# The position bias in the second attention: from TensorE to VectorE

## The chip, the cores and the metric

The kernel runs on one NeuronCore of a Trainium2 chip. The metric is the time of one execution on the device in microseconds (us). PE is TensorE, DVE is VectorE, ACT is ScalarE, POOL is GpSimd and SP is SyncE. PEld is the weight load of TensorE.

## The reference

One step of a two-layer diffusion backbone in fp32: 128 context tokens and 256 latent tokens (a grid of 4 rows by 64), width 1024. Layer 0 mixes tokens by differential attention, layer 1 by neighbourhood attention with 16 heads of 64; each is followed by an output projection, a layer norm, and a mixture of experts (32 experts, two per token). What matters here is the softmax of layer 1 for the latent tokens:

```
s_nb = einsum('bqhd,biqjhd->bhqij', q_r, k_nb) * scale
s_nb = s_nb + bias                       # learned, by head and offset; the window is 16 columns wide
s_ctx = einsum('bqhd,bphd->bhqp', q_r, k_ctx) * scale
p = softmax(concatenate([s_nb, s_ctx], -1))
```

The context tokens of that layer attend only to each other, without a bias.

## The kernel before, in words

All five engines have an instruction list written out by hand, and semaphores order them; no planner is at work. The stages follow each other: modulation, QKV projection, attention, output projection, layer norm, routing, experts; then layer 1 the same way.

Attention runs over 24 units, a unit being one tile of 128 queries and one pair of heads: `u // 8` is the tile `t` (0 the context, 1 and 2 the latent tokens), `u % 8` the pair `j`. A unit of tile 0 has 128 keys, one of tiles 1 and 2 has 384: the 128 of the context first, then the 256 latent ones. The 16 units of tiles 1 and 2 in layer 1 (`l == 1`) are the ones with a bias.

TensorE (`block.tensor`) issues, after three scores ahead, for each unit `u`: `transpose_prob(u)` (L787), `scores(u + 3)` (L769, and L776 for the bias), `attend(u - 1)` (L802, probabilities times values). The scores of both heads lie in two PSUM banks, and there are two such pairs of banks, so `scores(u)` waits for the exponentials of unit `u - 2`. In layer 1 the six transposes of a unit go into banks 4 and 5, which are not doubled: `transpose_prob(u)` waits until ACT has copied those of `u - 1` out. An fp32 matmul appears in the trace as two records, a transpose as one.

For the bias, PE multiplies the identity (`ident`) with a table `btab` in SBUF that holds, for every head, six runs of 64 columns: the bias shifted to its place and a very large negative number outside the window. It accumulates onto the scores of the latent keys, columns 128 to 384 of each bank. The table is made earlier in the layer (PE flips it, DVE adds the window at L1053).

DVE (`block.vector`) issues `maxima(u + 1)` (wait for the scores, then the negated maximum over the keys of both heads, L1067) and then `combine(u)`, which in layer 1 is only the reciprocal of the sums (L1077). When `u % 4 == 1` and `u >= 5` it issues `take_o`, which waits for the values matmuls of four units and writes half of an output tile (L1094). `chain(x)` issues x on DVE and then a drain, so that the next instruction of DVE starts only when x has written.

ACT (`block.scalar`) issues `exps(u + 2)` (two exponentials with their sums, L587; they wait for the maximum and for `transpose_prob(u)`, whose source buffer they overwrite) and then `take_pT(u)` (the transposed probabilities from PSUM to SBUF, L600). On POOL and SP nothing of the attention stage is waited for except that POOL loads the layer norm's rows when the last values matmul is done.

Of the kernel before, what the change touches and what calls it, by code (L numbers as in the profile page):

```python
# [20 lines left out]
P = 128  # L21
# [5 lines left out]
HD = 64  # L27
# [18 lines left out]
GRID_W = 64  # L46
NA_KH, NA_KW = 8, 16
ROWS = 256 // GRID_W
BM = 6
# [11 lines left out]
ALU = mybir.AluOpType  # L61
# [44 lines left out]
def backbone_kernel(nc, x_prompt, x_sample, cache_a_k, cache_a_v, cache_b_k, cache_b_v, c, c_ctx,  # L106
# [4 lines left out]
    with ctx:  # L111
# [3 lines left out]
        def overlay(tensors):  # L115

            with ExitStack() as s:
                return [s.enter_context(nc.sbuf_tensor(n, shape, dt)) for n, shape, dt in tensors]
# [4 lines left out]
        def sem2(name):  # L123
# [34 lines left out]
        qkv, hT, qT, kT, kctx, vctx, o = overlay([  # L158
            ("qkv", [P, NT, 3 * D], F32), ("hT", [P, KD, NT * P], F32), ("qT", [P, KD, NT * P], F32),
            ("kT", [P, KD, 4 * P], F32), ("kctx", [P, D], F32), ("vctx", [P, D], F32), ("o", [P, NT, D], F32)])  # L160
# [22 lines left out]
        ps = ps_t[:, :].rearrange("p (b n) -> p b n", b=8)  # L183
# [5 lines left out]
        ident = cst[:, C_ID:C_ID + P]  # L189
# [55 lines left out]
        def qkv_chunk(l, c):  # L245

            return QKV_B + c if l else QKV_A + c + 2 * min(c, KD)
# [11 lines left out]
        keys = [P, 3 * P, 3 * P]  # L259
        key0 = [0, P, P]  # L260
# [378 lines left out]
        def _(pe):  # L639
            mm = nc.tensor.matmul  # L640
# [57 lines left out]
            for kk in range(4):  # L698
                ins = nc.tensor.transpose(ps[:, 7, kk * P:(kk + 1) * P], mst[:, 0, kk * P:(kk + 1) * P], ident)
            ins.then_inc(mt_ps, 1)  # L700

            for l in range(LAYERS):
# [8 lines left out]
                for g in range(3):  # L711
# [3 lines left out]
                    for ck in range(4):  # L715
                        n = qkv_chunk(l, 4 * g + ck)
# [5 lines left out]
                    if l == 1 and g < 2:  # L722

                        pe.wait_ge(hank_ld, 32 * (g + 1))
                        for i in range(6):
                            f = 6 * g + i
                            if f >= 2:
                                pe.wait_ge(flip_used, f - 1)
                            mm(ps[:, 6 + f % 2, :], cst[:, C_FLIP:C_FLIP + P], hank[:, i * 512:(i + 1) * 512],
                               start=True, stop=True).then_inc(flip_done, 1)  # L730
# [8 lines left out]
                for j in range(PAIRS):  # L739
# [4 lines left out]
                    for t in range(NT):  # L744
                        ins = nc.tensor.transpose(ps[:, bq, t * P:(t + 1) * P], qkv[:, t, j * P:(j + 1) * P], ident)
# [3 lines left out]
                    for i in range(4):  # L749
                        ins = nc.tensor.transpose(ps[:, bk, i * P:(i + 1) * P], kin[i], ident)  # L750
# [11 lines left out]
                def scores(u):  # L762
                    t, j = u // PAIRS, u % PAIRS
                    if u >= 2:

                        pe.wait_ge(exp_done[l], u - 1)
                    biased = l == 1 and t > 0
                    for h in range(2):
                        ins = mm(ps[:, 2 * (u % 2) + h, 0:keys[t]],  # L769
                                 qT[HD * h:HD * (h + 1), j, t * P:(t + 1) * P],  # L770
                                 kT[HD * h:HD * (h + 1), j, key0[t]:key0[t] + keys[t]], start=True, stop=not biased)
                    if biased:
                        m0 = (2 - 2 * (t - 1)) * GRID_W
                        for h in range(2):
                            at = (2 * j + h) * BM * GRID_W + m0
                            ins = mm(ps[:, 2 * (u % 2) + h, P:keys[t]], ident, btab[:, at:at + ROWS * GRID_W],  # L776
                                     start=False, stop=True)
                    ins.then_inc(sc_done[l], 1)

                def transpose_prob(u):  # L780
# [25 lines left out]
                for u in range(3):  # L806
                    scores(u)
                for u in range(UNITS):
                    transpose_prob(u)
                    if u + 3 < UNITS:  # L810
                        scores(u + 3)
                    if u:
                        attend(u - 1)
# [5 lines left out]
                for cidx, nk in enumerate(WO_K):  # L819
                    n = WO0[l] + cidx  # L820
# [17 lines left out]
                for t in range(NT):  # L838
                    for k in range(KD):
                        ins = mm(ps[:, 6, t * w36:(t + 1) * w36], hT[:, k, t * P:(t + 1) * P], wr[:, l, k, :],  # L840
                                 start=(k == 0), stop=(k == KD - 1))
# [8 lines left out]
                for t in range(NT):  # L850
                    for i in range(t + 1):
                        mm(ps[:, 7, t * NE:(t + 1) * NE], tri if i == t else ones, a_all[:, i, :],
                           start=(i == 0), stop=(i == t))
                for t in range(NT):
                    ins = mm(ps[0:NE, 5, 0:1], a_all[:, t, :], ones[:, 0:1], start=(t == 0), stop=(t == NT - 1))
# [15 lines left out]
                for i in range(2 * NT):  # L871
                    ins = mm(ps[:, 1, 0:NBX], rt[:, 2400 + i * P:2400 + (i + 1) * P],
                             rt[:, 3200 + i * NBX:3200 + (i + 1) * NBX], start=(i == 0), stop=(i == 2 * NT - 1))
# [42 lines left out]
                with pe.Fori(0, n_act // HALVES) as pair:  # L916
                    for half in range(HALVES):
                        at = pair * HALVES + half
# [9 lines left out]
        def _(dve):  # L928
            v = nc.vector

            def chain(ins):

                dve.drain()
                return ins
# [90 lines left out]
            for l in range(LAYERS):  # L1025
# [35 lines left out]
                def maxima(u):  # L1061

                    t, j = u // PAIRS, u % PAIRS
                    n = keys[t]
                    sc = ps[:, 2 * (u % 2):2 * (u % 2) + 2, :]
                    dve.wait_ge(sc_done[l], u + 1)
                    v.tensor_reduce(negm[:, u % 2, :], sc[:, :, 0:n], AX, ALU.max, negate=True).then_inc(negm_rdy[l], 1)  # L1067

                def combine(u):
# [32 lines left out]
                def head_norm(q, step):  # L1102
# [17 lines left out]
                    else:  # L1120
                        chain(v.tensor_tensor(oh, oh, subg[:, :].unsqueeze(1).to_broadcast([P, 4, P]), ALU.mult))
                        if half:
                            dve.sem_inc(o_rdy[l], 1)

                maxima(0)
                for u in range(UNITS):
                    if u + 1 < UNITS:
                        maxima(u + 1)
                    combine(u)
                    q = (u - 5) // 4  # L1130
                    if u >= 5:
                        if u % 4 == 1:
                            take_o(q)
                        if l == 0:

                            for step in range(2 * ((u - 1) % 4), min(2 * ((u - 1) % 4) + 2, 7)):
                                head_norm(q, step)
# [214 lines left out]
```

## Time and profile before

| what | value |
|---|---|
| time, median of 3 runs | 1601.62 us (1598.58 to 1602.39) |
| the profiled execution's own time | 1598.8 us |
| its span, first to last instruction | 1597.0 us |
| mean granted TensorE clock | 0.853 of full |
| PE busy | 1110.6 us, 70% of the span |
| DVE busy | 404.2 us, 25% |
| ACT busy | 170.1 us, 11% |

Busy is the time in which the engine executed something; a granted clock of 1.00 is 2.4 GHz, 0.50 is 1.2 GHz. The second attention lies at about 988 to 1071 us of the span, the first at about 200 to 283. Times in rows are counted from the start of the span.

### The profile page before, as it was taken

The numbers are of one execution on the slowest core, as the hardware profiler recorded it, in microseconds if no ns is written. First come the engines' busy times: TensorE is split into PE (matmuls) and PEld (weight loads), VectorE is DVE, ScalarE is ACT, GpSimd is POOL, SyncE is SP. The second block draws the span as 40 slices with busy tenths as digits, with TensorE's granted clock in tenths as the row PEclk, the third lists the DMA queues.
The fourth block names the chain that finished last, engine by engine and source line by source line (L and its number), as shares of the span: only waits on it lengthen the run. The fifth ranks groups of instructions, "written<-read, shape, count | busy, mean of one in ns | idle before, by whom it ended". The sixth has DMA issues, their size and how long they took to land.

```text
span 1597.0 us, 25857 instructions
## 1 busy us (share of the span) xinstructions
PE 1110.6 (70%) x9606; PEld 587.1 (37%) x9607; DVE 404.2 (25%) x906; ACT 170.1 (11%) x460; POOL 210.9 (13%) x359
## 2 busy tenths in 40 slices
PE   3899977888448767865219998999426577877720
PEld 1333444424224433432114445774323234443310
DVE  0011177354201111110091112322741011111116
ACT  0110143001000000000000003440000000000000
POOL 0000000000112322331100000000002122322220
PEclk9899967896679988997659998899559689998975
DMA  8776300287699999999914423010039999699830
GB/s 330 267 263 251 94 25 1 103 311 311 267 423 388 424 423 426 381 425 424 422 56 141 123 79 105 1 51 3 40 133 409 424 426 424 246 423 384 359 150 40
DMA packets 84327, 398.26 MB, mean 249 GB/s; under 512 B 14656, under 2 KB 14944, under 8 KB 56640
## 3 DMA queue, kind: packets, MB, share of 16 engines
q1 hardware_dynamic: 61136, 341.91, 52.9%
q0 software_dynamic: 16240, 53.09, 9.1%
q10 hardware_dynamic: 6912, 2.76, 0.6%
q8 instruction: 22, 0.36, 0.1%
q14 instruction: 17, 0.14, 0.0%
HBM read 381.12 MB, written 16.72 MB: 249 GB/s over the span
## 4 chain that ended last, share of the span: by engine, by line
PE 44%; DMA 37%; DVE 10%; issue 3%; ACT 2%; DVEq 1%; SPq 1%; POOL 0%; ACTq 0%; POOLq 0%
PE ps L684 21%; DMA ring<-in_w_down_dram 20%; DMA ring<-in_w_up_dram 10%; PE ps L893 6%; PE ps L911 4%; DMA ring<-in_w_ada_dram 2%; PE ps L802 2%; DMA qkv<-ybuf 2%; PE ps L660 2%; PE ps L769 2%; DMA x<-in_x_sample_dram 1%; PE ps L840 1%; PE ps L787 1%; PE ps L776 1%; DMA ring<-in_w_gate_dram 1%
## 5 line engine op out<-in xcount | busy, mean ns | idle before, releaser
L893 PE MATMUL ps<-ring,xs 128*32 128x256 f32 x4736 | 313.9, 420 | 142.6 <-DMA ring<-in_w_up_dram 89.1
L893 PEld LDWEIGHTS ps<-ring,xs 128*32 128x32 f32 x4736 | 175.8, 119 | 273.1 <-issue 200.1
L684 PE MATMUL ps<-ring,hT 128*128 128x512 f32 x576 | 255.4, 604 | 5.3 <-ACT hT L536 4.2
L911 PE MATMUL ps<-ring,hm 128*32 128x256 f32 x2368 | 150.9, 393 | 36.7 <-ACT hm L630 27.1
L684 PEld LDWEIGHTS ps<-ring,hT 128*128 128x128 f32 x576 | 110.8, 194 | 148.8 <-issue 141.0
L1294 DVE TENSOR_TENSOR hp<-sg,ps 128x128 f32<-128x128 f32 x74 | 21.3, 288 | 330.1 <-ACT sg L627 330.1
L911 PEld LDWEIGHTS ps<-ring,hm 128*32 128x32 f32 x2368 | 69.4, 112 | 95.9 <-ACT hm L630 41.6
L1302 DVE COPY yo<-ps 128x256 f32<-128x256 f32 x74 | 31.4, 425 | 240.3 <-DMA ybuf<-yo,idy 161.4
L684 PE MATMUL ps<-ring,qT 128*128 128x512 f32 x192 | 84.9, 605 | 2.3 <-ACT qT L559 2.3
L627 ACT ACTIVATE sg<-ps 128x128 f32<-128x128 f32 x74 | 20.5, 277 | 616.0 <-PE ps L893 616.0
L451 POOL DMA_INDIRECT xg<-xmod,idx x78 | 77.3, 991 | 61.7 <-POOL idx L448 60.9
L461 POOL DMA_INDIRECT ybuf<-yo,idy x74 | 73.9, 999 | 61.1 <-POOL idy L458 58.2
L675 PE MATMUL ps<-cst,qkv 128*128 128x128 f32 x72 | 14.6, 376 | 79.7 <-DVE qkv L1013 55.1
L660 PE MATMUL ps<-ring,cond 128*32 128x512 f32 x384 | 53.6, 681 | 14.7 <-DMA ring<-in_w_ada_dram 14.7
L448 POOL COPY idx<-toki 128x1 int32 (+1 forms) x78 | 14.3, 183 | 364.9 <-DVE xs L1289 275.9
L900 PE MATMUL ps<-cst,hp 128*128 128x128 f32 x74 | 24.8, 335 | 52.9 <-DVE hp L1294 50.7
L587 ACT ACTIVATE hT<-ps,negm 128x384 f32<-128x384 f32 (+1 forms) x96 | 48.0, 505 | 83.7 <-DVE negm L1067 57.1
L684 PEld LDWEIGHTS ps<-ring,qT 128*128 128x128 f32 x192 | 37.2, 195 | 48.9 <-issue 46.1
L769 PE MATMUL ps<-kT,qT 64*128 64x384 f32 (+1 forms) x192 | 47.3, 582 | 4.0 <-ACT hT L587 2.3
L787 PE MATMUL ps<-cst,hT 128*128 128x128 f32 x168 | 33.7, 324 | 21.1 <-DVE hT L1085 18.2
L1289 DVE STREAM_TRANSPOSE xs<-xg 128x256 f32<-128x256 f32 x76 | 33.8, 445 | 55.7 <-DMA xg<-xmod,idx 55.5
L802 PE MATMUL ps<-qkv,hT 128*128 128x64 f32 (+1 forms) x240 | 46.6, 323 | 0.0
(194 smaller groups left out, 833.2 us busy)
## 6 DMA issues: line engine op xcount, KB each, us to landing
ring<-in_w_gate_dram SPq DMA_DIRECT2D x82, 1024.0 KB, 15.0
ring<-in_w_up_dram SPq DMA_DIRECT2D x82, 1024.0 KB, 15.2
ring<-in_w_down_dram SPq DMA_DIRECT2D x82, 1024.0 KB, 15.2
ring<-in_w_ada_dram SPq DMA_DIRECT2D x48, 1024.0 KB, 8.9
ring<-in_w_qkv_a_dram SPq DMA_DIRECT2D x12, 1024.0 KB, 5.1
ring<-in_w_qkv_b_dram SPq DMA_DIRECT2D x12, 1024.0 KB, 11.8
modb<-mdram POOLq DMA_DIRECT2D x12, 512.0 KB, 8.8
qkv<-ybuf POOLq DMA_DIRECT2D x2, 3072.0 KB, 15.6
```

The source lines that it names most:

```text
L451: pool.indirect_dma_start(out=xg[:, :], out_offset=None, in_=xmod.rearrange("r (j w) -> (r j) w", j=G), in_offset=bass.IndirectOffsetOnAxi ...
L461: pool.indirect_dma_start(out=ybuf.rearrange("r (j w) -> (r j) w", j=G), out_offset=bass.IndirectOffsetOnAxis(ap=idy[:, 0:1], axis=0), in_ ...
L587: ins = act.activation(e[:, h, 0:n], ps[:, 2 * (u % 2) + h, 0:n], ACT.Exp, bias=negm[:, u % 2, h:h + 1], accum_out=sums[:, u % 2, h:h + 1])
L660: ins = mm(ps[j * BLK:(j + 1) * BLK, ADA_BANK[i], :], cond[:, k, :], raw[:, n % RING, j * 512:(j + 1) * 512], start=False, stop=(k == KD - 1))
L684: ins = mm(ps[:, 2 * t + hf, :], lhs[:, k, t * P:(t + 1) * P], raw[:, slot, kk * D + hf * 512:kk * D + (hf + 1) * 512], start=(k == 0), st ...
L769: ins = mm(ps[:, 2 * (u % 2) + h, 0:keys[t]], qT[HD * h:HD * (h + 1), j, t * P:(t + 1) * P], kT[HD * h:HD * (h + 1), j, key0[t]:key0[t] + ...
L787: ins = nc.tensor.transpose(ps[:, 4 + (u % 2 if l == 0 else h), i * P:(i + 1) * P], prob[u % 2][:, h, i * P:(i + 1) * P], ident)
L802: ins = mm(tile_ps(3)[:, lo:lo + w], probT[u % 2][:, h, i * P:(i + 1) * P], values(t, i, lo, lo + w), start=(i == 0), stop=(i == nk - 1))
L893: ins = mm(ps[j * BLK:(j + 1) * BLK, 1, 0:W].rearrange("p (a n) -> p a n", a=2), xs[:, k, :], w[:, :, at:at + FW], start=(k == 0), stop=(k ...
L911: ins = mm(ps[j * BLK:(j + 1) * BLK, 5, 0:WD], hm[:, 2 * c + q, :], ring[:, slot + GU + c, q * D + j * WD:q * D + (j + 1) * WD], start=(c ...
L1289: v.transpose(xs[:, :, :].rearrange("p k n -> p (k n)"), xg[:, :]).then_inc(xs_rdy[l], 1)
L1302: v.tensor_copy(yo[:, :], ps[:, 5, 0:WD]).then_inc(yo_rdy[l], 1)
```

## The change

The matmuls with the identity go, and the matmul of the scores closes its own accumulation. DVE adds the same part of the table to the same columns of both banks, in place in PSUM, with one instruction for both heads, and drains before it takes the maximum.

```
@@ scores(u), TensorE
-                    biased = l == 1 and t > 0
                     for h in range(2):
                         ins = mm(ps[:, 2 * (u % 2) + h, 0:keys[t]],
                                  qT[HD * h:HD * (h + 1), j, t * P:(t + 1) * P],
-                                 kT[HD * h:HD * (h + 1), j, key0[t]:key0[t] + keys[t]], start=True, stop=not biased)
-                    if biased:
-                        m0 = (2 - 2 * (t - 1)) * GRID_W
-                        for h in range(2):
-                            at = (2 * j + h) * BM * GRID_W + m0
-                            ins = mm(ps[:, 2 * (u % 2) + h, P:keys[t]], ident, btab[:, at:at + ROWS * GRID_W],
-                                     start=False, stop=True)
+                                 kT[HD * h:HD * (h + 1), j, key0[t]:key0[t] + keys[t]], start=True, stop=True)
                     ins.then_inc(sc_done[l], 1)
@@ maxima(u), VectorE
                     dve.wait_ge(sc_done[l], u + 1)
+                    if l == 1 and t > 0:
+                        m0 = (2 - 2 * (t - 1)) * GRID_W
+                        bias = btab[:, 2 * j * BM * GRID_W:2 * (j + 1) * BM * GRID_W].rearrange("p (h n) -> p h n", h=2)
+                        chain(v.tensor_tensor(sc[:, :, P:n], sc[:, :, P:n], bias[:, :, m0:m0 + ROWS * GRID_W], ALU.add))
                     v.tensor_reduce(negm[:, u % 2, :], sc[:, :, 0:n], AX, ALU.max, negate=True).then_inc(negm_rdy[l], 1)
```

## Rows read from the trace of the kernel before

**Rows 1.** Busy time of each engine by stretch: us, (x instructions), PEclk, DMA share, GB/s.

```profile
core 0: us, PE busy (x) PEld busy (x) DVE busy (x) ACT busy (x) POOL busy (x), PEclk, DMA share, GB/s
1018.00:1034.00 16.00, 15.85 (x107) 12.40 (x106) 4.81 (x9) 7.80 (x21) 0.00 (x0) 1.00 0.01 1
1050.00:1070.70 20.70, 18.74 (x145) 16.19 (x143) 3.95 (x8) 9.35 (x22) 0.00 (x0) 1.00 0.00 1
```

**Rows 2.** The chain of waits through one plain unit: start us, us, what.

```profile
1022.25 0.66 PE ps L787 x6
1022.91 0.85 PE ps L769 x4
1023.75 1.06 PE ps L776 x4
1024.82 1.28 PE ps L802 x12
```

**Rows 3.** Groups of instructions, 1000 to 1072 us: busy, mean ns, idle before, releasers.

```profile
L776 PE MATMUL ps<-btab,cst 128*128 128x256 f32 x64 | 19.0, 422 | 0.0
L1067 DVE TENSOR_REDUCE negm<-ps 128x2 f32<-128x768 f32 x16 | 15.3, 958 | 27.0 <-PE ps L776 26.3 <-issue 0.4
```

**Rows 4.** The chain of waits around the output at 1045 us.

```profile
1042.42 0.85 PE ps L769 x4
...
1045.65 0.69 DVE o L1094
1046.34 0.03 DVEq L1097
...
1046.54 0.97 DVE negm L1067
...
1048.77 0.71 ACT hT L600
1049.47 0.14 issue
1049.61 0.84 PE ps L787 x6
1050.45 0.85 PE ps L769 x4
```

**Rows 5.** The timeline: start us, us, engine, instruction, [idle before, releaser].

```profile
1024.85 0.96 DVE L1067 TENSOR_REDUCE negm<-ps 128x2 f32<-128x768 f32 x1 [2.82 <-PE ps L776]
...
1050.55 0.58 ACT L587 ACTIVATE hT<-ps,negm 128x384 f32<-128x384 f32 x1 [1.09 <-PE ps L787]
...
1051.68 0.81 ACT L600 ACTIVATE hT<-ps 128x768 f32<-128x768 f32 x1
```

**Rows 6.** DVE groups by shape over the span, then two chained instructions of the timeline.

```profile
L1053 DVE TENSOR_TENSOR btab<-ps,cst 128x512 f32<-128x512 f32 x12 | 8.3, 692 | 84.4 <-PE ps L729 84.3
L1094 DVE TENSOR_TENSOR o<-ps,rsum 128x512 f32<-128x512 f32 x12 | 8.3, 691 | 29.5 <-PE ps L802 29.5
L1007 DVE TENSOR_TENSOR qkv<-t,modb 128x1024 f32<-128x1024 f32 x6 | 11.6, 1926 | 0.5
...
225.81 0.69 DVE L1109 TENSOR_TENSOR t<-o 128x512 f32<-128x512 f32 x1
226.58 0.69 DVE L1111 TENSOR_REDUCE var<-t 128x4 f32<-128x512 f32 x1
```

**Rows 7.** The chain of waits through the first biased units.

```profile
1001.45 1.58 PE ps L769 x4
1003.03 2.00 PE ps L776 x4
...
1008.95 0.85 PE ps L769 x4
...
1014.93 0.85 PE ps L769 x4
```

**Rows 8.** Busy time by stretch again: the first attention, and the start of the biased units.

```profile
204.00:286.00 82.00, 63.19 (x263) 39.89 (x263) 64.35 (x180) 33.54 (x112) 2.08 (x4) 0.69 0.02 7
...
258.00:262.00 4.00, 1.75 (x11) 1.02 (x11) 3.22 (x13) 1.61 (x5) 0.00 (x0) 1.00 0.00 0
...
266.00:270.00 4.00, 3.13 (x12) 1.43 (x10) 3.56 (x9) 2.37 (x8) 0.00 (x0) 0.50 0.00 0
...
1006.00:1008.00 2.00, 2.00 (x9) 1.23 (x9) 0.10 (x2) 1.51 (x5) 0.00 (x0) 0.84 0.00 0
```

## Prediction

> **What bounds the kernel now.** I read the chain of waits for the stretch of the second attention first, then the busy time of the engines by stretch, then the groups of instructions, and last the timeline where the chain leaves TensorE. The stretch that the change touches runs from the first biased scores at 1001.45 us [rows 7] to 1070.7. In it PE is busy for 15.85 of 16.00 us from 1018 and 18.74 of 20.70 from 1050, DVE for 4.81 and 3.95, DMA for next to nothing [rows 1]. The chain stays on PE: transposes of the probabilities 0.66, scores 0.85, bias 1.06, values 1.28 us, so one unit (a head pair of a query tile) takes 3.85 us [rows 2]. DVE only waits there: 26.3 us until the bias matmuls end [rows 3]. The reader should see that PE is the bound of a plain unit, that the other engines have slack, and that every fourth unit the chain leaves PE for DVE and ACT [rows 4].
>
> **What goes.** 32 matmuls with the identity, recorded as 64 (two for each), 19.0 us of PE records at 422 ns [rows 3]. Records overlap, so I price by the chain: 1.06 us per unit at full clock, 2.00 us for the first unit, which runs at half [rows 2, 7]. Sixteen units: 2.0 + 15 x 1.06 = 17.9 us of PE time. That is the ceiling, not the gain. Their weight loads go too; they lie beside the matmuls.
>
> **What comes.** Sixteen in-place adds of 128 x 512 on DVE, ahead of the maximum, with a drain between. No row shows a DVE instruction that reads and writes PSUM. The nearest, 512 elements from PSUM plus SBUF into SBUF, takes 692 ns, and so does the one of L1094 [rows 6]. Below that nothing speaks for less. From above I take the dearest two-operand form by its elements: 1926 ns for 1024 with a broken-up pattern [rows 6] is 0.96 us for 512. I take 0.69, since both operands here run in two straight pieces. With the drain the maximum starts 226.58 - 225.81 = 0.77 us after the add [rows 6]. Sixteen of them are 12.3 us of DVE time, in an engine with over 10 of 16 us idle. What matters is only how late the maximum becomes.
>
> **A plain unit afterwards.** PE alone would need 0.66 + 0.85 + 1.28 = 2.79 us. But a second loop is close behind. The transposes of a unit wait for the copy that ACT made of the previous unit's; ACT's exponentials for two units on wait for those transposes, since they reuse the buffer; and the copy stands behind the exponentials on ACT. One turn can be read where the chain passes through it: the copy ends at 1048.77 + 0.71 = 1049.48, PE begins to transpose at 1049.61 [rows 4], ACT begins the exponentials at 1050.55 and ends the next copy at 1051.68 + 0.81 = 1052.49 [rows 5]. So 3.01, say 3.02 us. A plain unit saves 3.85 - 3.02 = 0.83 us, not 1.06. Does the add fit? Count from the start of the scores: they end at 0.85, DVE starts 0.03 later (24.82 + 0.03 [rows 2, 5]), 0.77 for the add, 0.96 for the maximum [rows 5], 0.03 to ACT: 2.64. ACT wants it 3.02 + 0.10 = 3.12 after the start of the scores (1050.55 against 1050.45 [rows 4, 5]). Slack 0.48 us, so the add costs nothing here, also at the upper bound of 0.96 us. Queued behind it on DVE are only the reciprocal and, every fourth unit, the output of the sums.
>
> **Every fourth unit.** DVE then takes the output half from PSUM (0.69 us), waiting for the values matmuls of a unit ago, and the next maximum stands behind it [rows 4]. Before, the start of that wait is 0.85 + 1.06 + 1.28 = 3.19 after the scores, the maximum ends 1.86 after DVE begins (1045.65 to 1047.51), and the next scores but one start late by little: 1050.45 - 1042.42 = 8.03 against 7.70, a loss of 0.33 us. After, the wait ends at 0.85 + 1.28 = 2.13; 0.03 and 0.69 for the output, 0.20 until DVE is free (1046.54 - 1046.34), 0.77 and 0.96 for add and maximum, 0.03 to ACT: 4.81, where ACT wanted it at 3.12. The loop has no slack of its own, so these 1.69 us are all on the path: the unit takes 4.71 instead of 4.18. Each costs 0.53 us against before. This is the wait that takes the place of the matmuls.
>
> **Sum.** I count intervals between the starts of the scores of two units; the biased ones are 8 to 23. From unit 13 on there are eight plain intervals: 8 x 0.83 = 6.6; and two with an output: 2 x -0.53 = -1.1. The first four intervals (units 8 to 12, 1001.45 to 1014.93, 13.48 us [rows 7]) still have short transposes and values; the last two take 5.98, so 2.99 us each, and run at the ACT loop already. In the first, at half clock, the bias is in the way for 2.00 us; I give 1.8, less a little for the second. The interval after it, with the first output, gains 0.3 by the same walk (clock and buffers are as before), and the tail with the last output 0.2. Together 6.6 - 1.1 + 1.8 + 0.3 + 0.2 = 7.8 us at an unchanged clock. The add at its upper bound takes 0.27 more at four outputs: 6.7.
>
> **The clock.** The granted clock is half, 1.2 GHz, when the biased units begin; the first scores take 1.58 us instead of 0.85. It rises to 2.4 GHz in 1006 to 1008 (mean 0.84 [rows 8]), and is 1.00 from 1018 on, where PE is busy almost without gaps [rows 1, 7]. Afterwards PE would be busy for 4 x 2.79 = 11.2 of 4 x 3.02 + 1.69 = 13.8 us, 81%, with a gap at each output. In the first attention PE was busy for 63.19 of 82.00 us and its clock was 0.69 on average, so half for (1 - 0.69) / 0.5 = 62% of the time: full from 258 to 262 with PE busy for 1.75 us, half from 266 to 270 with 3.13 [rows 8]. On the other side 1050 to 1070.7 kept the full clock with PE idle for 2.0 us. At half, a unit takes about 2.79 x 1.58 / 0.85 = 5.2 us instead of 3.02, so each us at half loses 0.42. I take 4 to 5 us more at half than before (a rise that comes a little later, or one fall), 1.9 us, and keep 0 and 6 us of loss for the range. The page "TensorE: Matmul & The Clock Gate" of the Trainium skill, section "A second HAM failure mode: psum-queue depth-cycling", says that short idle spells of the PE between groups of matmuls can make its clock swing between the levels. By that rule the second attention would become like the first, and the change would be slower. The first attention agrees with that rule, the stretch from 1050 to 1070.7 does not [rows 1, 8].
>
> **After the attention** nothing hides the gain: the output projection and all that follows wait for its end in series, DMA is idle in the stretch [rows 1], and the weights of that projection do not keep it waiting. So 7.8 - 1.9 = 5.9 us reach the end. The profiled execution took 1598.8 us, 1.8 more than its span of 1597.0; it becomes 1592.9. The median of the runs shown is 1601.62, 2.8 above; I forecast for it: 1595.7 us.
>
> **Rivals.** (1) The clock is lost. Place: from the second biased unit to the end. For it: the first attention [rows 8], the gap of about 1.7 us at every output, and the place of the change: the removed matmuls ran just where the clock rose. Against: 81% busy is more than in the first attention. It decides from 7.8 / 0.42 = 19 us more at half. With 30 us, most of what the stretch then lasts for, it costs 12.6 - 7.8 = +4.8: 1606.4. Chance 0.15. (2) DVE becomes the bound because in-place access to PSUM is dear, say twice the nearest row, 1.38 us. Then ACT wants the maximum 0.21 us sooner than it comes in eight plain units, and at four outputs it comes 0.69 later still: 7.8 - 1.7 - 2.8 = 3.3, less 1.9 for the clock: 1600.2. Against: every plain DVE form of 512 elements lies at 0.69. Chance 0.12. (3) PE was the only bound and the ACT loop is looser than I read: 8 x 0.23 = 1.8 more, 1593.9 or less. Against: the turn was read at one place, but without a gap in it. Chance 0.08. (4) The change doesn't do what it says, PE being off the path: against it stand the chain and 26.3 us of DVE waiting; 1601.6, chance 0.03.
>
> **How the numbers follow.** The forecast has 0.62, its own range 1592.5 to 1599.5. The whole range, 1590.5 to 1603, takes in the lower loss of clock with the looser loop, and the dear add; it leaves out most of the first rival. What a measurement can tell from no change is 0.3%, 4.8 us, that is below 1596.8 for faster. The forecast is faster in about three of four cases; with rival 3 and little of the others: 0.54. Slower than 1606.4 is the worse half of the first rival, and a little of unknown causes: 0.09. The rest, 0.37, is the same.
>
> **What would show it.** Right: score starts 3.0 us apart in plain units with the exponentials following the transposes without a wait for DVE; 4.7 us at outputs, with ACT waiting for the maximum; the add at 0.69 us; sixteen DVE adds and no bias matmuls. Wrong: half clock in the stretch beyond 1012 us for more than a few us, adds well over 0.7 us, or plain units at 2.8 or at 3.3 and more.

## The result: slower by 0.4%, and the profile after

The changed kernel takes 1607.09 us (median of 20 runs, 1602.27 to 1612.03), the kernel before 1600.88 (20 runs, 1593.63 to 1607.38). The ratio is 1.0042, 95% interval 1.0028 to 1.0057: 6.2 us slower, where 5.9 us faster were forecast. It is the first rival, given 0.15 and 1606.4 us.

The profiled execution: span 1603.1 us, against 1597.0. First the busy time by stretch, for the kernel before over the stage from its first biased scores to its last values (us, busy and (x instructions) of PE, PEld, DVE, ACT, POOL, then the granted clock, DMA share and GB/s).

```profile
1001.45:1070.68 69.23, 66.98 (x438) 52.73 (x439) 20.20 (x40) 32.77 (x87) 0.00 (x0) 0.96 0.01 1
```

The same view of the kernel after: the stage, and the stretches that answer to those before [rows 1, 8].

```profile
998.12:1075.10 76.98, 72.17 (x374) 54.43 (x374) 31.40 (x56) 32.77 (x87) 0.00 (x0) 0.70 0.00 1
...
204.00:286.00 82.00, 58.70 (x272) 36.74 (x272) 66.34 (x188) 34.99 (x120) 2.08 (x4) 0.77 0.03 11
...
1003.00:1018.00 15.00, 15.00 (x58) 10.45 (x59) 7.42 (x13) 5.64 (x17) 0.00 (x0) 0.50 0.01 2
1018.00:1034.00 16.00, 14.33 (x96) 10.20 (x95) 8.31 (x14) 9.07 (x25) 0.00 (x0) 0.93 0.00 1
1034.00:1050.00 16.00, 16.00 (x64) 11.80 (x63) 5.18 (x9) 4.29 (x12) 0.00 (x0) 0.50 0.00 1
1050.00:1070.70 20.70, 17.56 (x127) 15.19 (x125) 7.78 (x14) 10.98 (x27) 0.00 (x0) 0.91 0.00 1
```

The stage is 7.75 us longer. PE executes 64 records fewer in it (374 for 438) and is busy for 5.2 us longer. The reader should see the granted clock: 0.70 for 0.96. A mean of 0.70 is (1 - 0.70) / 0.5 = 60% of 77 us at half, 46 us; before it was 8% of 69, 5.5 us. (The first attention, whose code is the same, went from 0.69 to 0.77; in the fourteen traces of this case it lies between 0.67 and 0.77, so it varies by itself.) From 1034 to 1050 PE is busy for 16.00 of 16.00 us, and all of it at 1.2 GHz: a full row of PE is not a sign that PE works at its rate.

Now the chain of waits after, which answers to the plain unit and to the output before [rows 2, 4]: a plain unit at full clock, the output, and a unit at half clock.

```profile
1021.44 0.84 PE ps L768 x4
1022.28 1.48 PE ps L795 x12
1023.76 0.69 PE ps L780 x6
1024.46 0.84 PE ps L768 x4
...
1026.82 0.69 DVE o L1091
...
1027.64 0.70 DVE ps L1063
...
1028.41 0.97 DVE negm L1064
...
1030.63 0.71 ACT hT L600
1031.34 0.14 issue
1031.48 0.85 PE ps L780 x6
1032.32 0.93 PE ps L768 x4
1033.25 2.75 PE ps L795 x12
1036.00 1.28 PE ps L780 x6
1037.28 1.58 PE ps L768 x4
1038.87 2.75 PE ps L795 x12
```

L768 are the scores, L795 the values, L780 the transposes. At full clock the scores are 1024.46 - 1021.44 = 3.02 us apart. At half they are 2.75 + 1.28 + 1.58 = 5.61 apart, where the kernel before needed 3.85 with the bias in them. The clock fell just behind the output, about 1.5 us after PE had waited 1.67 us. Now the tail, behind the last output. The busy time by stretch after, with PE idle for 2.71 us and then at half clock:

```profile
1063.00:1067.00 4.00, 1.29 (x13) 1.19 (x12) 1.04 (x3) 2.13 (x6) 0.00 (x0) 1.00 0.00 0
1067.00:1071.00 4.00, 4.00 (x22) 4.00 (x22) 0.00 (x0) 1.42 (x2) 0.00 (x0) 0.51 0.00 0
```

The chain of waits from the last values to the first matmul of the output projection (L684), before and then after:

```profile
1068.06 2.63 PE ps L802 x24
...
1074.56 5.85 PE ps L684 x13
```

```profile
1070.09 5.01 PE ps L795 x24
...
1080.03 4.99 PE ps L684 x11
```

The half clock runs on behind the stage: from its end to the projection are 1080.03 - 1075.10 = 4.9 us, where they were 1074.56 - 1070.68 = 3.9. Last, the new DVE group, over the span.

```profile
L1063 DVE TENSOR_TENSOR ps<-ps,btab 128x512 f32<-128x512 f32 x16 | 11.2, 700 | 18.2 <-PE ps L768 17.4 <-issue 0.4
```

### The profile page after: what moved, and what is told of

Its sections match the earlier page's. It is cut to its first block, busy times and chain, and to the rows that moved or that the text cites. A ratio compares the mean times of both kernels' runs of the same rounds, so it can differ in the third digit from the quotient of the medians.

```text
span 1603.1 us, 25761 instructions
## 1 busy us (share of the span) xinstructions
PE 1116.5 (70%) x9542; PEld 586.7 (37%) x9543; DVE 415.3 (26%) x922; ACT 170.3 (11%) x460; POOL 211.0 (13%) x359
## 4 chain that ended last, share of the span: by engine, by line
PE 45%; DMA 36%; DVE 10%; issue 3%; ACT 2%; DVEq 1%; SPq 1%; POOL 0%; ACTq 0%; POOLq 0%
PE ps L684 21%; DMA ring<-in_w_down_dram 17%; DMA ring<-in_w_up_dram 12%; PE ps L886 7%; PE ps L904 4%; PE ps L795 3%; DMA ring<-in_w_ada_dram 2%; DMA qkv<-ybuf 2%; PE ps L660 2%; PE ps L768 2%; DMA x<-in_x_sample_dram 1%; PE ps L780 1%; PE ps L833 1%; DVE negm L1064 1%; DVEq L926 1%
## 5 line engine op out<-in xcount | busy, mean ns | idle before, releaser
L886 PE MATMUL ps<-ring,xs 128*32 128x256 f32 x4736 | 319.9, 426 | 139.5 <-DMA ring<-in_w_up_dram 86.2
L684 PE MATMUL ps<-ring,hT 128*128 128x512 f32 x576 | 254.2, 602 | 5.3 <-ACT hT L536 4.2
L684 PEld LDWEIGHTS ps<-ring,hT 128*128 128x128 f32 x576 | 110.3, 193 | 148.1 <-issue 140.3
L1291 DVE TENSOR_TENSOR hp<-sg,ps 128x128 f32<-128x128 f32 x74 | 21.3, 288 | 333.2 <-ACT sg L627 333.2
L684 PE MATMUL ps<-ring,qT 128*128 128x512 f32 x192 | 84.7, 603 | 2.2 <-ACT qT L559 2.2
L780 PE MATMUL ps<-cst,hT 128*128 128x128 f32 x168 | 37.0, 351 | 26.8 <-DVE hT L1082 20.9
L684 PEld LDWEIGHTS ps<-ring,qT 128*128 128x128 f32 x192 | 37.0, 194 | 48.9 <-issue 46.0
L795 PE MATMUL ps<-qkv,hT 128*128 128x64 f32 (+1 forms) x240 | 53.2, 358 | 0.0
L768 PE MATMUL ps<-kT,qT 64*128 64x384 f32 (+1 forms) x192 | 49.9, 610 | 4.0 <-ACT hT L587 2.3
L795 PEld LDWEIGHTS ps<-qkv,hT 128*128 128x128 f32 x240 | 45.1, 262 | 10.3 <-issue 10.2
```

The source lines that it names most:

```text
L684: ins = mm(ps[:, 2 * t + hf, :], lhs[:, k, t * P:(t + 1) * P], raw[:, slot, kk * D + hf * 512:kk * D + (hf + 1) * 512], start=(k == 0), st ...
L768: ins = mm(ps[:, 2 * (u % 2) + h, 0:keys[t]], qT[HD * h:HD * (h + 1), j, t * P:(t + 1) * P], kT[HD * h:HD * (h + 1), j, key0[t]:key0[t] + ...
L780: ins = nc.tensor.transpose(ps[:, 4 + (u % 2 if l == 0 else h), i * P:(i + 1) * P], prob[u % 2][:, h, i * P:(i + 1) * P], ident)
L795: ins = mm(tile_ps(3)[:, lo:lo + w], probT[u % 2][:, h, i * P:(i + 1) * P], values(t, i, lo, lo + w), start=(i == 0), stop=(i == nk - 1))
L886: ins = mm(ps[j * BLK:(j + 1) * BLK, 1, 0:W].rearrange("p (a n) -> p a n", a=2), xs[:, k, :], w[:, :, at:at + FW], start=(k == 0), stop=(k ...
```

## Experiments

Two questions were open: is the loss the clock, or the longer way through DVE; and if it is the clock, is it the gap of PE at the outputs or the smaller amount of PE work. "Stage" below is from the first biased scores to the last values, in the one profiled execution. Ratios are to the kernel before in the same series, whose medians were 1602.18 and 1602.27 us.

**The changed kernel, two more profiled executions.** No edit.

> The changed kernel once more, one look, to see how far its clock differs from one execution to the next. Theory CLOCK: half for a good part of the stage again, mean granted clock 0.6 to 0.85 in it, stage 68 to 80 us, and the units at full clock 3.02 us apart, those at half 5.6. A clock of 0.95 with a stage of 77 us would be against it.

> The changed kernel a third time, one look: a mean clock of 0.6 to 0.85 in the stage and falls that follow outputs, at other outputs than in the two looks so far; stage 68 to 80 us.

Measured: 1611.60 and 1612.32 us; stages of 74.2 and 74.8 us at a mean clock of 0.78 and 0.75, so 33 and 37 us at half. Both are in the expected ranges. One expectation failed: the falls came at no other outputs than before. In all three executions one followed the second output of the stage and one the last; one of the three had a fall at the third as well. In the first of the two, the busy time by stretch around two outputs and what came behind them (columns as above):

```profile
1032.00:1036.00 4.00, 2.33 (x19) 1.97 (x18) 3.09 (x6) 1.93 (x5) 0.00 (x0) 1.00 0.00 0
1036.00:1042.00 6.00, 6.00 (x27) 4.57 (x27) 1.73 (x3) 2.25 (x6) 0.00 (x0) 0.55 0.00 0
1052.00:1056.00 4.00, 3.42 (x17) 2.31 (x17) 1.60 (x4) 2.37 (x6) 0.00 (x0) 0.71 0.00 0
1056.00:1060.00 4.00, 4.00 (x17) 2.83 (x16) 0.54 (x2) 1.18 (x5) 0.00 (x0) 0.50 0.01 4
```

The gap comes first, then the half clock, with PE busy all the time.

**The kernel before, a second profiled execution.** No edit.

> The kernel before once more, one look, for the spread of its stage: clock 0.93 to 0.97 and 69 to 71 us expected.

Measured: 69.1 us, clock 0.97. The three stages after, 77.0, 74.2 and 74.8, have a mean of 75.3; less 69.2 that is 6.1 us. With the 1.1 us behind the stage (4.9 for 3.9 in all three, against both of the kernel before) it is 7.2, and the medians differ by 6.2, with an interval of 4.5 to 9.1. So no other cause is needed, though three executions can't exclude one of a microsecond or two: in the same changed kernel the stage begins at 998.1, 1004.5 and 1004.8 us, and nothing ahead of it was changed. The 6.1 us lie in two places. Up to the last scores the stage is 2.5 us longer (59.1 for 56.6), and from the last scores to the last values 3.7 us (16.3 in each of the three, for 12.6 in both).

**Filler in the place of the bias matmuls.**

```
# scores(u), l == 1 and t > 0, ahead of the scores
+   for h in range(2):
+       for _ in range(2):
+           mm(ps[:, 2 * (u % 2) + h, 384:512], ident, btab[:, 384:512], start=True, stop=True)
```

> Edit: the changed kernel, and ahead of the scores of each biased unit PE again runs as many columns through the identity as the removed bias matmuls had (two of 128 columns for each head), but into the 128 spare columns of the scores' bank, which nothing reads. DVE still adds the bias. Theory CLOCK (the removed matmuls had kept PE busy enough for the full clock; without them it falls to half): the granted clock is as in the kernel before, 0.9 or more over the stage from the first biased scores to the last values, plain units are 3.85 us again, outputs cost about 0.75 us more each than before; stage 71 to 73 us against 69.2 before and 77.0 after; time 1602 to 1605, below the changed kernel although PE does more. Theory DVE (the add in front of the maximum is what costs): the stage stays at 77 or gets longer, time 1607 or more.

Measured: 1613.22 us (12 runs), ratio 1.0054 (1.0034 to 1.0074); stage 74.6 us at a clock of 0.93. The clock went as the clock theory said and the units too: 3.88 us plain, 4.88 and 4.96 with an output, against 4.10 and 4.18 before. The time did not: it is no better than the changed kernel. The miss of the stage is in its tail, 17.2 us from the last scores to the last values for 12.6 before. Behind the last output PE idled and the clock was lost here too:

```profile
1063.00:1067.00 4.00, 1.27 (x11) 1.16 (x11) 1.67 (x4) 1.93 (x5) 0.00 (x0) 0.98 0.00 0
1067.00:1071.00 4.00, 4.00 (x21) 4.00 (x20) 0.00 (x0) 0.81 (x1) 0.00 (x0) 0.50 0.00 0
```

Two parts lie outside the stage: the projection begins 1.7 us later behind it, at half clock, and the filler of the first biased unit runs ahead of it, where the context units take 15.6 us for 13.9. Together 5.4 + 1.7 + 1.7 = 8.8 us over the kernel before; the ratio says 8.6 (5.4 to 11.9).

So the add on DVE costs something at the outputs whatever the clock does, 0.78 us each, and a clock that is held by work in the way of the scores is paid for with that work. This run alone doesn't decide between the two theories.

**The output one maximum later.**

```
# DVE, the loop over units
-   if u >= 5:
-       if u % 4 == 1:
+   if l == 1 and u >= 6 and u % 4 == 2:
+       take_o(q)
+   if u >= 5:
+       if l == 0 and u % 4 == 1:
            take_o(q)
```

> Edit: the changed kernel, with the output half in the second attention taken one maximum later, so that the maximum no longer queues behind it on DVE. The gap of PE at every fourth unit should go. Theory CLOCK: with the gaps gone the clock should not fall once it is full, so the stage is 77 less 4 x 1.7 and less what the half clock after the gaps took: 60 to 68 us, time 1592 to 1600; if the clock stays at half for long even without gaps, what it looks at is how much PE works in a unit and not the gaps, and the stage is 70 or more. Theory DVE queue (the wait behind the output is all of the loss): 4 x 1.7 = 6.8 us less, stage 70, time 1600, with the clock as in the changed kernel.

> The changed kernel with the output one maximum later once more, one look: if no gap means no fall, again every full-clock unit at 3.02 us, no half clock after the first rise, stage 56 to 59 us.

Measured: 1590.63 us (6 runs), ratio 0.9919 (0.9891 to 0.9948), and 1595.97 in the second profiled execution, beside one of the kernel before at 1603.82. The stages are 57.25 and 57.2 us at a clock of 0.90 in both, for the first of them less than either theory expected. The chain of waits of the first, where an output now lies inside:

```profile
1030.22 0.85 PE ps L768 x4
1031.07 1.48 PE ps L795 x12
1032.55 0.69 PE ps L780 x6
1033.24 0.85 PE ps L768 x4
1034.09 1.48 PE ps L795 x12
1035.57 0.70 PE ps L780 x6
1036.27 0.85 PE ps L768 x4
1037.11 1.48 PE ps L795 x12
1038.59 0.70 PE ps L780 x6
1039.29 0.85 PE ps L768 x4
```

Every unit takes 3.02 us and the chain never leaves PE. The busy time by stretch of the same run: half until the clock rises, then full to the end.

```profile
1004.75:1016.00 11.25, 11.25 (x39) 6.29 (x38) 5.55 (x10) 5.17 (x19) 0.00 (x0) 0.50 0.01 2
1018.00:1062.00 44.00, 42.99 (x326) 34.39 (x325) 23.94 (x43) 26.79 (x67) 0.00 (x0) 1.00 0.01 1
```

The stage is 18 us shorter than the mean of the changed kernel. The delay at four outputs explains at most 4 x 1.9 = 7.6 (4.93 - 3.02 at the longest); the rest is the clock. This is also the version that beats both kernels.

**The same order in the kernel before.**

> Edit: the kernel before (bias by PE matmuls), with the output half in the second attention taken one maximum later. It asks how much of the gain of the late output belongs to the order alone. Theory GAPS (the late output gains where it closes gaps that let the clock fall; before, there are hardly any): three intervals lose 0.33, 0.25 and 0.28 us and the tail 1 us; stage 67 to 68.5 us, time 1599 to 1601. Theory ORDER (taking the output later is worth 10 us in any kernel): 1592.

Measured: 1600.38 us (12 runs), ratio 0.9982 (0.9960 to 1.0005); stage 67.5 us, clock 0.96. This is what theory GAPS expected. The order alone is worth at most some 6 us and likely 2. The gain of 12 to 13 us over the kernel before belongs to the two changes together.

**Filler in the gaps only.** Nothing of the delay is taken away.

```
# PE, the loop over units, behind attend(u - 1)
+   if l == 1 and u >= 9 and u % 4 == 1:
+       at = ((u - 1) % PAIRS + 1) * P
+       for _ in range(3):
+           mm(tile_ps(3)[:, at:at + 3 * P], ident, btab[:, 0:3 * P], start=True, stop=True)
```

> Edit: the changed kernel, the order of DVE untouched; PE fills its gap at each of the four outputs with three matmuls of the identity over 384 spare columns of the output bank, about 1.3 us at full clock, which nothing reads. The wait of ACT for the maximum stays. Theory CLOCK BY GAPS: the clock no longer falls after an output; it still begins at half, so 65 to 72 us for the stage and 1598 to 1603 in time, 4 to 9 less than the changed kernel. Theory DELAY (the maximum behind the output costs the time itself, idle PE does not matter): the filler changes nothing or adds to the path, 1607 to 1612.

Measured: 1597.98 us (12 runs), ratio 0.9971 (0.9946 to 0.9995); stage 64.7 us, clock 0.91. The output units still take 4.97 to 4.98 us. (The filler was sized wrong: it takes 2.15 us at full clock, not 1.3, so it overfills the gap.) Twelve matmuls that compute nothing make the changed kernel 9 us faster by the medians and 11 by the two ratios; the stage is 10.6 us shorter. The delay theory wanted 1607 or more. The busy time by stretch:

```profile
1000.00:1010.00 10.00, 10.00 (x36) 5.78 (x36) 4.85 (x9) 4.87 (x15) 0.00 (x0) 0.50 0.01 2
1010.00:1062.67 52.67, 51.95 (x360) 39.64 (x360) 25.41 (x44) 26.83 (x68) 0.00 (x0) 1.00 0.00 1
```

**Filler in the context units**, to begin at full clock: alone, with the filler in the gaps, and with the late output.

```
# scores(u), l == 1 and t == 0, ahead of the scores
+   for h in range(2):
+       mm(ps[:, 2 * (u % 2) + h, 128:512], ident, btab[:, 128:512], start=True, stop=True)
```

> Edit: the changed kernel, and ahead of the scores of the eight context units of layer 1 (no bias, 128 keys) PE runs the identity over 384 spare columns of each of the two banks, which nothing reads. Theory CLOCK: the clock is full when the biased units begin (it is half there before and after), the context stage takes no longer than its 13 us, and the first biased units run at 3.0 us; outputs still open gaps, after which it may fall. Stage 62 to 72 us against 77.0 after, time 1594 to 1602. Theory DVE: nothing before the stage matters to it, 77 us, and the context units get longer by up to 0.8 us each: 1607 or more.

> Edit: the same filler at the four outputs, and the filler in the eight context units. Theory CLOCK BY GAPS: full clock from the first biased unit to the last values: 16 units of 3.02 and four outputs at 1.7 to 1.9 more: stage 60 to 65 us, time 1594 to 1598. Theory DELAY: 1607 or more.

> Edit: the two edits before this one together: the output one maximum later, and filler matmuls in the eight context units. Theory CLOCK: full clock through the whole stage, every unit at the loop of 3.02 us: 16 units, stage 55 to 60 us, 10 to 14 us less than before; time 1587 to 1592. Theory DVE: stage 70, time 1600.

Measured, in this order: 1608.07 us (12 runs), ratio 1.0045 (1.0020 to 1.0070); 1599.51 us (12 runs), 0.9980 (0.9956 to 1.0004); 1591.92 us (9 runs), 0.9926 (0.9902 to 0.9951). The stages:

```profile
1001.86:1066.72 64.86, 55.22 (x374) 43.11 (x374) 31.67 (x56) 32.82 (x87) 0.00 (x0) 0.94 0.01 1
```

```profile
1003.88:1066.38 62.50, 59.13 (x399) 43.77 (x399) 31.68 (x56) 32.82 (x87) 0.00 (x0) 1.00 0.00 1
```

```profile
1009.07:1064.15 55.08, 52.73 (x375) 40.36 (x375) 31.15 (x54) 32.82 (x87) 0.00 (x0) 0.97 0.01 1
```

The filler does what it should: the clock is full when the biased units begin. It brings no time over the kernels without it (0.9980 for 0.9971, 0.9926 for 0.9919). The stage is 2.2 us shorter, but the filler costs more than that ahead of it: the context units together take 16.8 us in all three, for 13.0 to 14.0 in the ten without filler there or in the biased units. In the third the clock was not full all through, as had been expected: it fell once, for 3.4 us, behind a gap of 1.1 us among the first biased units. Alone it does not help at all: the gaps are there, and the median is where the changed kernel's is. The clock theory expected 1594 to 1602 us here and missed (the other theory's 1607 or more holds), and the trace can't explain it: the profiled execution, at 1600.27 us next to the fastest, passed gaps of 1.68 and 1.75 us at full clock and lost it only in the tail.

**No bias at all.** The `tensor_tensor` in `maxima` is taken out as well.

> Edit: the changed kernel without the add on DVE, so that the bias and the window are left out altogether and only the removal is seen. The experts chosen afterwards differ, so only the stage from the first biased scores to the last values counts, not the total. Theory CLOCK BY GAPS: plain units stay at 3.02 us (the loop over ACT doesn't hold the add); at the outputs the maximum comes 0.77 us sooner, unit about 3.95, gap about 0.9 us instead of 1.7; the clock is lost less or not at all: mean 0.8 to 0.97, stage 57 to 66 us. Theory WORK (what counts is how much PE does per unit, not gaps): same clock as in the changed kernel, 0.70 to 0.78, stage 70 us or more.

Measured: stage 69.2 us, clock 0.77; output units of 4.07 and 4.16. By stretch: the start, the middle, and behind the last two outputs.

```profile
999.51:1020.00 20.49, 20.49 (x75) 13.00 (x74) 6.71 (x14) 8.75 (x28) 0.00 (x0) 0.50 0.00 1
1020.00:1056.00 36.00, 34.12 (x251) 26.16 (x248) 13.15 (x24) 20.48 (x53) 0.00 (x0) 0.99 0.00 1
1056.00:1064.00 8.00, 6.07 (x32) 5.96 (x32) 0.60 (x3) 2.98 (x7) 0.00 (x0) 0.64 0.00 0
```

This was a miss for the theory of gaps, which expected 57 to 66 us; the clock is in the range of theory WORK (0.70 to 0.78), and the stage just below its 70 us. What the run shows is a second part of the mechanism. For 20 us PE was busy without a break at half clock, and the clock did not rise; with the bias matmuls it rose 5 us into the stage. Taking the matmuls away makes the clock rise late, also without any add. The other traces agree: with the bias matmuls it rose 4.8 to 5.5 us into the stage, three times in three; without them and without filler up to there, 11.5 to 21.3 us into it, seven times in seven. The gap makes it fall again: with the gaps at the outputs cut to half of their length, 0.90 and 0.98 us, none was followed by a fall, and the one fall came in the tail, in a gap of 1.93 us.

## Why the prediction was wrong

**The mechanism in the units was right.** A plain unit takes 3.02 us, the number of the ACT loop, not the 2.79 of PE alone. The add takes 0.70 us (0.69 was taken), and in plain units it costs nothing. The unit with an output takes 4.85 to 4.93 us where it lies wholly at full clock, forecast 4.71. Rivals 2, 3 and 4 are out.

**The sum at an unchanged clock was somewhat too large.** With the clock at 1.00 all through, and outputs lengthened by the filler to 4.97, the stage is 62.5 us, so 6.7 less than 69.2, at a clock a little better than before's; 7.8 was forecast. The largest error is the first interval with an output: it was to gain 0.3 on its 4.12, and it took 4.97 there, 4.76 and 4.96 in the second and third executions of the changed kernel. The two later ones cost 0.75 each where 0.53 was taken.

**The clock failed, and it alone turned the sign.** The step was "I take 4 to 5 us more at half than before", with 6 us of loss as the end of the range. Measured were 46, 33 and 37 us at half, 39 in the mean, for some 5 before: 34 more. The forecast said that the balance tips at 19 us. The price of one was nearer: 75.3 less the 62.5 of the kernel that keeps its clock is 12.8 us, over 39 is 0.33, forecast 0.42. That is a mean of two prices: the 12 us before the rise cost 2.2 us (64.7 with them, 62.5 without), 0.18 each, and the other 27 cost 10.6, 0.40 each. A plain unit all at half takes 5.61 us, where 5.2 was taken. So what was mis-sized was the amount, and there were two mistakes in it. The rise was taken as nearly given, though the prediction itself had seen that the removed matmuls ran just where it came; it came 5 us into the stage before, and 21.3, 11.6 and 12.3 us into it after. That is 10 of the 34 us. The falls are the other 24. And one gap of 2.0 us that had passed without a fall [rows 1] was set against a first attention at half for 62% of its time [rows 8], as if they weighed the same. Four longer gaps, each with its own chance of a fall, and each fall followed by several units of 5.6 us, are another thing than one gap near the end.

The tail failed the same way: its last output was booked as a gain of 0.2 us. With the clock held by filler it was about that (12.5 for 12.6 us). In the changed kernel PE waited 2.71 us there, the clock fell in all three executions, and it cost 3.7 us in the stage and 1.1 behind it. That the outcome lies within 1 us of the first rival's 1606.4 is in part luck: the rival took fewer us at half, 30, at a higher price, 0.42, and set a larger gain against them, 7.8.

The Trainium skill's rule on short idle spells ("TensorE: Matmul & The Clock Gate", section "A second HAM failure mode: psum-queue depth-cycling") should have had more weight: the clock did swing between the levels as it says, and with the gaps at the outputs closed, twice by the order and twice by filler, once full it did not fall in the stage in any of the four traces. In the fifth, with the late output and the context filler, it fell once, early.

**Open.** How long a gap may be for the clock to stay isn't settled. At the outputs of the stage, at full clock, the fourteen traces have these: 0.72 to 0.98 us, eleven gaps and no fall behind them; 1.59 to 1.78 us, eight gaps and four falls; 1.93 to 1.96 us, three gaps and one fall; 2.70 to 2.73 us, five gaps and five falls. Elsewhere it also fell behind shorter ones: behind two of 0.9 and 1.1 us close together as the context units begin, in the eleven traces without filler there, and behind one of 1.1 us among the first biased units. Why half-clock stretches differ from one execution to the next (46, 33, 37 us) isn't either. Whether the late output has the same clock in every execution isn't shown either: two of them were profiled.

## What to carry to other kernels

Work taken from PE is worth what the next loop leaves of it (here 0.83 of 1.06 us a unit), and then only if PE stays busy: price each new gap as a possible fall of the clock, with the units at half behind it, before it is booked as slack. The last gap of a stage counts for more than its length, since the half clock behind it runs on into the next stage (here 1.1 us). When an engine's in-order list puts a longer chain in front of what PE waits for, move what nobody is waiting for behind it; here one reordered instruction turned 0.4% slower into 0.8% faster. In the trace read the granted clock beside the busy time, since at half clock PE looks busier than at full.

## What the runs showed of the hardware

- An in-place `tensor_tensor` of 128 x 512 fp32 in PSUM, second operand in SBUF, takes 700 ns, as good as the 692 from PSUM into SBUF [rows 6].
- PE was busy for 20.49 of 20.49 us at half clock without the clock rising, in transposes, scores over 64 rows and values of 64 columns; with the bias matmuls among them it had risen 5 us into the stage.
- At the outputs, longer gaps of PE were followed by a fall of its clock more often: none of eleven gaps below 1 us, four of eight at 1.6 to 1.8 us, five of five at 2.7 us. One execution of the changed kernel passed a gap of 1.78 us and fell behind one of 1.68.
- Matmuls whose result nobody reads, 12 of them in four gaps, were worth 9 to 11 us.
- At half clock the twelve values matmuls of a unit take 2.75 us in the chain, the six transposes 1.28 and the scores 1.58, against 1.28, 0.66 and 0.85 at full [rows 2].
